# Expert outputs by way of DRAM rows and indirect transfers, in place of scatter products

## The reference

```python
def moe_swiglu(h, w_router, w_gate, w_up, w_down):
    t = h.reshape(-1, d)
    logits = jnp.dot(t, w_router, preferred_element_type=jnp.float32)
    top_val, top_idx = lax.top_k(logits, TOP_K)                      # 2 of 8
    gates = jax.nn.softmax(top_val, axis=-1)
    combine = jnp.sum(jax.nn.one_hot(top_idx, N_EXPERTS) * gates[..., None], axis=1)
    out = jnp.zeros_like(t)
    for e in range(N_EXPERTS):
        out = out + combine[:, e:e + 1] * swiglu(t, w_gate[e], w_up[e], w_down[e])
    return out
```

## Time and profile before

| | us |
|---|---|
| runs | 1451.43, 1448.97, 1451.37 |
| median | 1451.37 |
| profiled execution, span from first to last instruction | 1449.6 |
| PE busy in it | 1406.7 |
| DVE busy | 1159.7 |
| ACT busy | 960.5 |

### The profile page before, as it was taken

One profiled execution on the slowest core, in us unless ns is written; L12 is line 12 of the kernel. 1 busy time (PEld: TensorE's weight loads), 2 busy tenths in 40 slices (PEclk: granted clock), 3 DMA queues, 4 the chain that ended last, 5 costly groups with the idle time before them and its releaser, 6 DMA issues.

```text
span 1449.6 us, 17894 instructions
## 1 busy us (share of the span) xinstructions
PE 1406.7 (97%) x6623; PEld 1155.5 (80%) x6623; DVE 1159.7 (80%) x1063; ACT 960.5 (66%) x841; POOL 9.1 (1%) x51
## 2 busy tenths in 40 slices
PE   7979999999989999999999999999999999999998
PEld 5757788887867888888888888878888888888886
DVE  6884554446686899998898899888889989888986
ACT  5584534344575777777777777767777777777774
POOL 2000000000000000000000000000000000000000
PEclk9999999999999999999999999999999999999999
DMA  8405655365504999999999999989999999999993
GB/s 279 159 30 204 222 183 180 119 232 174 174 8 154 332 380 367 355 377 375 334 353 377 364 358 377 376 297 379 371 366 355 376 358 325 377 377 344 376 369 117
DMA packets 181600, 421.52 MB, mean 291 GB/s; under 512 B 9241, under 2 KB 12365, under 8 KB 181517
## 3 DMA queue, kind: packets, MB, share of 16 engines
q1 hardware_dynamic: 178460, 418.56, 80.5%
q0 software_dynamic: 560, 1.59, 0.4%
q10 hardware_dynamic: 2496, 0.23, 0.1%
HBM read 419.28 MB, written 1.06 MB: 290 GB/s over the span
## 4 chain that ended last, share of the span: by engine, by line
PE 86%; DVE 8%; ACT 3%; issue 2%; DMA 1%; ACTq 0%; DVEq 0%; SPq 0%
PE ps L1753 27%; PE ps L1755 26%; PE ps L1754 26%; PE ps L2211 2%; DVE w_lo L1511 1%; DVE w_lo L1090 1%; DVE work L1199 1%; DVE h L1640 1%; PE ps L2177 1%; ACT w_hi L939 1%; PE ps L2189 0%; PE ps L2188 0%; DMA router<-in_od_router_dram 0%; DMA h<-in_x_dram 0%; ACT w_hi L673 0%
## 5 line engine op out<-in xcount | busy, mean ns | idle before, releaser
L1511 DVE TENSOR_TENSOR w_lo<-raw,w_hi 128x2048 fp32r<-128x2048 f32 x336 | 768.3, 2290 | 105.8 <-ACT w_hi L939 105.1
L939 ACT ACTIVATE w_hi<-raw 128x2048 fp32r<-128x2048 f32 x336 | 644.8, 1919 | 242.7 <-PE ps L1755 242.6
L1753 PE MATMUL ps<-w_hi,xT_hi 128*128 128x512 f32 (+2 forms) x1312 | 514.9, 392 | 10.5 <-DVE w_lo L1090 3.0
L1755 PE MATMUL ps<-w_hi,xT_lo 128*128 128x512 f32 (+2 forms) x1312 | 507.7, 387 | 0.0
L1754 PE MATMUL ps<-w_lo,xT_hi 128*128 128x512 f32 (+2 forms) x1312 | 507.4, 387 | 0.0
L1753 PEld LDWEIGHTS ps<-w_hi,xT_hi 128*128 128x128 f32 x1312 | 247.0, 188 | 64.2 <-issue 6.1
L1755 PEld LDWEIGHTS ps<-w_hi,xT_lo 128*128 128x128 f32 x1312 | 246.8, 188 | 50.6
L1754 PEld LDWEIGHTS ps<-w_lo,xT_hi 128*128 128x128 f32 x1312 | 247.1, 188 | 47.2
L1090 DVE TENSOR_TENSOR w_lo<-raw,w_hi 128x2048 fp32r<-128x2048 f32 (+4 forms) x65 | 138.3, 2137 | 102.4 <-ACT w_hi L673 102.3
L1753 PE MATMUL ps<-w_hi,hT_hi 128*128 128x512 f32 (+1 forms) x548 | 215.4, 393 | 2.0 <-DVE hT_lo L1104 2.0
L1754 PE MATMUL ps<-w_lo,hT_hi 128*128 128x512 f32 (+1 forms) x548 | 213.6, 390 | 0.0
(11 more groups left out here) (288 smaller groups left out, 646.6 us busy)
## 6 DMA issues: line engine op xcount, KB each, us to landing
raw<-in_od_ex_gate_dram SPq DMA_DIRECT2D x112, 1024.0 KB, 5.9
raw<-in_od_ex_up_dram SPq DMA_DIRECT2D x112, 1024.0 KB, 6.0
raw<-in_od_ex_down_dram SPq DMA_DIRECT2D x112, 1024.0 KB, 5.8
raw<-in_od_w_qkv_dram SPq DMA_DIRECT2D x12, 1024.0 KB, 5.4
raw<-in_ev_ff_gate_dram SPq DMA_DIRECT2D x10, 1024.0 KB, 5.4
raw<-in_ev_ff_up_dram SPq DMA_DIRECT2D x10, 1024.0 KB, 5.1
raw<-in_ev_ff_down_dram SPq DMA_DIRECT2D x10, 1024.0 KB, 5.0
raw<-in_ev_w_in_dram SPq DMA_DIRECT2D x5, 1024.0 KB, 9.1
```

The costliest lines, as they stand in the source:

```text
L939: act.activation(w_hi[:, (DENSE + q) % SPLIT, :], raw[:, r, :], ACT.Copy).then_inc(hi_ready, 1)
L1511: dve.tensor_tensor(w_lo[:, k, :], raw[:, raw_of(DENSE + q), :], w_hi[:, k, :].bitcast(F32), ALU.subtract).then_inc(lo_ready, 1)
L1753: pe.matmul(out, x_hi, hi, start=start, stop=False)
L1755: return pe.matmul(out, x_lo, hi, start=False, stop=stop)
```

## The change

Results of experts 0 to 6 no longer pass through scatter products. ACT copies each result from PSUM as plain float32 rows (`y_rows`), and SP stores them to a DRAM table `row_scratch` of 7 x 128 rows, in the next expert ahead of load 12. In expert 0 DVE works out, for each token and each of its two choices, the row number in that table and the weight (`row_places` at step 7, `row_lists` at step 13); the weight is 0 where the choice is expert 7. When the seventh store has landed, in expert 7, POOL issues four indirect transfers (two choices, two halves of the tokens), each of 128 rows of 4 KB, into `hg` and `xs`, which are free by then. DVE adds them into `h` with four operations in expert 7, two at step 24 and two at step 30. Expert 7 itself (and spare runs) still go by selection and scatter products. PE no longer waits for `scatter_read` in the experts, but waits for the copies (`rows_ready`) ahead of an expert's first down unit.

```diff
+ROWS_STORE = 12
+ROWS_ADD = 24
...
+        y_rows = sb("y_rows", [P, D])
+        row_base = sb("row_base", [P, 1, E])
+        row_sums = sb("row_sums", [P, 4, TT])
+        row_index = sb("row_index", [P, 2, TT], I32)
...
+        row_scratch = nc.dram_tensor("row_scratch", (E - 1, P, D), F32, kind="Internal").ap()
...
@@ sync: load_expert @@
                 for q, (kind, j, u) in enumerate(EXPERT):
+                    if q == ROWS_STORE and rows_ahead:
+                        sp.wait_ge(rows_ready, 2 * i)
+                        sp.dma_start(row_scratch[bass.ds(i - 1, 1), :, :].rearrange("e p d -> p (e d)"), y_rows[:, :]).then_inc(rows_stored, 16)
...
@@ scalar @@
+            def output_rows(i, first):
+                act.wait_ge(y_psum, i + 1)
+                if not first:
+                    act.wait_ge(rows_stored, 16 * i)
+                for nn in range(2):
+                    if nn:
+                        act.wait_ge(unit_used, i * len(EXPERT) + (DENSE + len(EXPERT)))
+                    act.activation(y_rows[:, nn * N:(nn + 1) * N], ps[:, 6 + nn, :], ACT.Copy).then_inc(rows_ready, 1)
...
                     for q in range(SPLIT - 1):
                         split_unit(i, q)
-                    outputs(i - 1)
+                    output_rows(i - 1, second)
                     split_unit(i, SPLIT - 1)
...
-                    if q == LAST_UP and even:
-                        turn_selection(p + 1)
+                    if q == LAST_UP and scattered:
+                        turn_selection(1)
...
@@ vector @@
+            def row_places():
+                dve.tensor_scalar(row_base[:, 0, :], slots_f[:, 0:E], float(P), None, ALU.mult).then_inc(vec_chain, 1)
+                chain[0] += 1
+                link(dve.scalar_tensor_tensor(out=g[:, 3, :, :], in0=rank[:, :, 0:E], scalar=float(P), in1=comb[:, :, 0:E],
+                                              op0=ALU.is_lt, op1=ALU.mult))
+                link(dve.scalar_tensor_tensor(out=g[:, 0, :, :], in0=rank[:, :, 0:E], scalar=float(P - 1),
+                                              in1=row_base[:, :, :].to_broadcast([P, TT, E]), op0=ALU.min, op1=ALU.add))
+                for m, hot in enumerate((2, 5)):
+                    dve.tensor_tensor(g[:, 1 + 3 * m, :, :], g[:, hot, :, :], g[:, 0, :, :], ALU.mult)
+                    ins = dve.tensor_tensor(g[:, 7 + m, :, :], g[:, hot, :, :], g[:, 3, :, :], ALU.mult)
+                link(ins)
+            def row_lists():
+                for m in range(2):
+                    dve.tensor_reduce(row_sums[:, m, :], g[:, 1 + 3 * m, :, 0:E - 1], AX.X, ALU.add)
+                    ins = dve.tensor_reduce(row_sums[:, 2 + m, :], g[:, 7 + m, :, 0:E - 1], AX.X, ALU.add)
+                link(ins)
+                dve.tensor_copy(row_index[:, :, :], row_sums[:, 0:2, :]).then_inc(rows_placed, 1)
+            def add_rows(m):
+                dve.wait_ge(rows_back, 16 * 2 * TT)
+                if m:
+                    dve.wait_ge(rows_added, TT)
+                for t in range(TT):
+                    dve.scalar_tensor_tensor(out=h[:, t, :], in0=(hg, xs)[m][:, t, :], scalar=row_sums[:, 2 + m, t:t + 1], in1=h[:, t, :],
+                                             op0=ALU.mult, op1=ALU.add).then_inc(rows_added, 1)
...
                 if begun:
-                    for q in range(SPLIT - 1):
+                    for q in range(SPLIT):
                         split_unit(i, q)
-                    outputs(i - 1)
-                    split_unit(i, SPLIT - 1)
...
+                        if q == 7:
+                            row_places()
...
+                        if q == 13:
+                            row_lists()
...
-                    if begun:
-                        if 1 <= q <= 4:
-                            add_scattered(i - 1, q - 1)
-                        if q == 6:
-                            dve.wait_ge(scatter_read, 4 * i)
+                    if adds and q in (ROWS_ADD, ROWS_ADD + 6):
+                        add_rows((q - ROWS_ADD) // 6)
...
-                        dve.wait_ge(selT_psum, p + 1)
+                        dve.wait_ge(gather_psum, 4 * p + 4)
...
@@ tensor: expert @@
-                    elif begun:
-                        pe.wait_ge(scatter_read, 4 * (i - 1) + 2 + j + 1)
-                    if j == ECH - 1 and even:
-                        pe.wait_ge(selT_ready, p + 1)
+                    if j == ECH - 1 and scattered:
+                        pe.wait_ge(selT_ready, 1)
...
                         pe.wait_ge(hT_ready, i * ECH + j + 1)
+                        if j == 0 and begun:
+                            pe.wait_ge(rows_ready, 2 * i)
...
-                        if j == 1 and u == 0 and begun:
-                            pe.wait_ge(scatter_read, 4 * (i - 1) + (kind == "up") + 1)
...
-                    if q == 1 and begun:
-                        scatter(i - 1, p if even else p + 1, 1 if even else 0)
...
-                    if q == LAST_UP and even:
+                    if q == LAST_UP and scattered:
                         turn_selection(2)
...
-            scatter(E - 1, PAIRS, 1)
+            scatter(0, 1)
...
@@ gpsimd @@
+            pool.wait_ge(rows_placed, 1)
+            pool.wait_ge(rows_stored, 16 * (E - 1))
+            row_table = row_scratch.rearrange("e p d -> (e p) d")
+            for m in range(2):
+                for t in range(TT):
+                    pool.indirect_dma_start((hg, xs)[m][:, t, :], None, row_table,
+                                            bass.IndirectOffsetOnAxis(row_index[:, m, t:t + 1], 0)).then_inc(rows_back, 16)
```

More of the change, by code:

```diff
@@ L424, in trunk @@
         scatter_read = sem("scatter_read")
+        rows_ready = sem("rows_ready")
+        rows_stored = sem("rows_stored")
+        rows_placed = sem("rows_placed")
+        rows_back = sem("rows_back")
+        rows_added = sem("rows_added")
         stored = sem("stored")
@@ L578, in load_expert @@
                     sp.dma_start(dst, src.rearrange("e p k n -> p (e k) n")).then_inc(landed[r], 16)
-            load_expert(0, 0)
+            load_expert(0, 0, False)
             with sp.Fori(1, E) as i:
@@ L591, in spare @@
                     e = sp.value_load(over_i[0:1, n:n + 1], min_val=0, max_val=E - 1)
-                    load_expert(E + n, e)
+                    load_expert(E + n, e, False)
                     if n + 1 < SPARE:
@@ L601, in _ @@
                 v = slice(nn * N, (nn + 1) * N)
-                sp.wait_ge(scatter_read, 4 * (n_over + E) - (3 - n))
+                sp.wait_ge(scatter_read, 4 * (n_over + 1) - (3 - n))
                 sp.dma_start(out[0, t * P:(t + 1) * P, v], h[:, t, v]).then_inc(stored, 16)
@@ L971, in turn_selection, with expert @@
                 act.activation(selT[:, :, :], ps[:, 4, :].rearrange("p (s n) -> p s n", s=2), ACT.Copy).then_inc(selT_ready, 1)
-            def expert(i, even, p, begun, gathers):
+            def expert(i, even, p, begun, gathers, second=False, scattered=False):
                 first = i * len(EXPERT) + DENSE
@@ L1038, in _ @@
             expert(0, True, 0, False, False)
-            expert(1, False, 0, True, True)
+            expert(1, False, 0, True, True, second=True)
             act.wait_ge(routed, 1)
@@ L1044, in _ @@
                 expert(p * 2 + 1, False, p, True, True)
-            expert(E - 2, True, PAIRS - 1, True, False)
+            expert(E - 2, True, PAIRS - 1, True, False, scattered=True)
             expert(E - 1, False, PAIRS - 1, True, False)
@@ L1051, in spare @@
                 with act.If(n_over > n):
-                    turn_selection(PAIRS + n + 1)
+                    turn_selection(n + 2)
                     for half in range(2):
@@ L1626, in gathered_lo, with outputs @@
                                 ps[:, bank:bank + 2, :].rearrange("p b (c n) -> p (b c) n", n=T)).then_inc(x_lo_ready, 1)
-            def outputs(i):
+            def outputs(n):
                 for nn in range(2):
-                    dve.wait_ge(y_hi_ready, 2 * i + nn + 1)
+                    dve.wait_ge(y_hi_ready, 2 * n + nn + 1)
                     v = slice(nn * N, (nn + 1) * N)
                     dve.tensor_tensor(y_lo[:, v], ps[:, 6 + nn, :], y_hi[:, v].bitcast(F32), ALU.subtract).then_inc(y_lo_ready, 1)
+            def row_places():
[22 more added lines that the diff above has]
+                                             op0=ALU.mult, op1=ALU.add).then_inc(rows_added, 1)
             def add_scattered(i, n):
@@ L1638, in add_scattered @@
                 v = slice(nn * N, (nn + 1) * N)
-                dve.wait_ge(scatter_psum, 4 * i + n + 1)
-                dve.scalar_tensor_tensor(out=h[:, t, v], in0=ps[:, 2 + n, :], scalar=comb[:, t, bass.ds(i, 1)], in1=h[:, t, v],
+                dve.wait_ge(scatter_psum, 4 * (i - (E - 1)) + n + 1)
+                dve.scalar_tensor_tensor(out=h[:, t, v], in0=ps[:, 2 + n, :], scalar=comb[:, t, i:i + 1], in1=h[:, t, v],
```

(33 more changed lines are left out.)

2 lines of the change are left out of this document (1 added, 1 removed).

## The result

| | before | after |
|---|---|---|
| median of 4 runs, us | 1450.71 | 1437.78 |
| range, us | 1448.97 to 1451.43 | 1436.20 to 1437.88 |
| profiled execution: its time, us | | 1436.2 |
| its span, us | 1449.6 | 1434.1 |

The ratio of the runs compared is 0.9904, with a 95% interval from 0.9892 to 0.9916: about 1% less time, and the interval excludes 1. The medians lie 12.9 us apart, where 13.6 us were forecast. In the whole study two executions stand far outside, one of the kernel before (2020.76 us) and one with the gathers twice (7888.72 us), and they enter no ratio.

A forecast was written before the change was run, and what follows sets the result against it. PE was taken to set the time: -12.95 (scatters) - 1.29 (turned selections) - 2.5 (waits for h) + 3.0 (sums) + 0.1 (row numbers) = -13.6 us, from the median 1451.37 to 1437.8 us; range 1433 to 1445 us.

The forecast's parts named there:

- PE is the bound, and time off PE counts.: Expert stage: PE loses seven scatters (12.95 us), three turned selections (1.29) and seven waits for h (2.5), counted in full.
- DVE gets less to do, so it doesn't become the pace.: Changes of experts: DVE loses two remainders and four additions, has 102.5 us of gaps; PE's 16.7 us count in full.
- Row numbers.: Expert 0, ahead of prod: DVE's row_places and row_lists, nearly covered by its lead, cost 0.1 us; 1.5 us without cover.
- Sums.: Expert 7, steps 24 and 30: each pair of additions takes 2.4 us against 0.87 us cover; PE stalls 3.0 us altogether.
- Store and gathers at nothing.: Stores behind each expert and four indirect transfers in expert 7 are hidden by the lead of the loads; cost 0.
- the lead shrinks by a few us and holds: Expert 7: with the gathers, 46.7 MB to move; the loads' 9.7 us to spare shrinks slightly but still covers; cost 0.
- landings near 6 us: Sign that the forecast is right: loads still land near 6 us after issue, with SP still waiting for DVE.
- (a): Rival: transfers become the pace, with today's mean of 361 GB/s as the ceiling; about 1467 us, chance 0.04.
- (b): Rival: gathered rows come late in expert 7, holding DVE at step 24, then PE; 1476 us at 25 each, chance 0.06.
- (c): Rival: freed time returns as DVE waits (sums, units 2 or 3, POOL slowing DVE); 4 to 10 us lost, chance 0.13.
- (d): Rival: PE does less, but each change of experts lasts as long, a remainder being late; 1449 to 1452 us, chance 0.05.
- (e): Rival: the sums are covered too and DVE's relief speeds up more; 1431 to 1434.5 us, chance 0.04.

The follow-up runs named there:

- e0: Period of expert 0, from PE's first gather product to ACT's first copy of its result: 123.88 us before, 123.84 after; difference -0.04, forecast -0.33.
- e7: Period of expert 7, from ACT's first copy of the previous result to its first copy into y_hi: 119.54 us before, 120.66 after; forecast difference +0.79.
- e1: Period of expert 1, between ACT's first copies of successive experts' results: 123.84 us before, 121.49 after; difference -2.35, forecast -2.21.
- the idle products: Changed kernel with eight unread products of a scatter's size put back on PE behind unit 1 of experts 1 to 7; 1450.60 us.
- the sums apart: Changed kernel with the four sums of rows one each in steps 22, 28, 34 and 40 instead of two pairs; 1434.44 us.

## Why the prediction was right, and where it was off

The mechanism and the sizes held, but that the median met 1437.8 us to 0.02 us is luck. The forecast counted from 1451.37 us, the median of three runs, and the four runs have 1450.71; and over the expert stage costs 0.62 us above forecast in e0 and e7 stand against gains 0.35 us above it in e1 to e6.

**PE is the bound, and time off PE counts.** Right, and shown: the idle products took back 1.88 us each, up to the time before. The three sizes hold: scatter 1.88 (forecast 1.85), wait for h 0.40 (0.36) and turn 0.40 (0.43), the last two by subtraction.

**"DVE gets less to do, so it doesn't become the pace."** Right, but narrower than it reads. The argument was DVE's 102.5 us of gaps, a sum over the stage. With its old work DVE would have been the pace at each shorter change, for 0.62 us, 4.3 in all. The relief was a condition of the full gain, not a side effect; of the 4.3 us the prediction had counted 2.5, as the waits for h.

**Row numbers.** Forecast 0.1 us. In expert 0 `row_places` stands from 489.59 to 490.55 us ahead of prod, and PE's next unit starts late once, at 493.49 (0.38 us after the product before it, then 0.34, where 0.46 is usual for the two): 0.26 us. With the turn's 0.4 us gone, that leaves most of e0's -0.04 explained, and some 0.1 us not.

**Sums.** The mechanism, the place and the only two stalls were as forecast; the size was 3.4 us against 3.0, the difference being mostly the slower product behind each stall (0.11) and the pair's 2.47 us where 2.4 were taken (the earlier trace rows has 2.5 busy for its two). Shown by the sums apart.

**Store and gathers at nothing.** Right in effect (no gathers: 0.05 us; a second store: none), though the sizes were off, which the time to spare hid. The store lands after 7.0 to 9.3 us, not about 4, since it queues with the loads; a gather lands after 8.9 to 9.8, not 4.2, and its issue takes 2.3 to 2.9, not the 0.53 of the earlier trace rows. Of 63.6 us from the store's issue (1313.82) to the first sum, 27 are used. The step that was too easy is "the lead shrinks by a few us and holds": loads land after 7 us in the median instead of 5.9, and after up to 12.7 us in expert 7, so of the 9.7 us to spare about 3 were left, and double the gathers overran it. The sign "landings near 6 us" did not come.

**Rivals.** (a) is refuted at this size: where the transfers did become the pace they ran at about 400 to 410 GB/s, not at the 361 of the mean before. The Trainium skill's 358 GB/s (HBM Reference, Specifications (TRN2)) is no limit for this core alone, which the same section also says. (b) is a true mechanism that needs rows later by 37 us; forced, it cost 14.4 us. (c) did not come at its price of 4 to 10 us: no unit 2 or 3 was late and POOL didn't slow DVE; its first part came in small, 0.4 us at the sums. (d) is refuted by the periods. (e) did not come, but is what the sums apart reach, at 1434.44.

## What to carry to other kernels

When work is taken off the bounding engine at one place, look there for what its neighbour had been hiding under it: here 0.62 us of DVE a change would have shown, where 0.36 had shown before, had the same edit not taken it away as well. An operation put into an engine's in-order stream should be shorter than that engine's lead at that step; four pieces of 1.28 us were free where two of 2.47 us cost 3.4. A detour through DRAM is free as long as the lead of the other transfers covers it, so look at how late they land against that lead: here landings of 12.7 us of a lead of 15.6 cost nothing, and with 2.1 MB more they reached 17.8 and cost 1.7 us.

## What the runs showed of the hardware

- An indirect transfer of 128 rows of 4 KB cost POOL 0.94 to 1.01 us to issue with DVE standing and 2.27 to 2.90 us beside DVE's remainders, which read two inputs from SBUF; DVE lost nothing.
- A 512 KB store into DRAM, issued among the loads, landed after 8.5 us (median), twice what POOL's 512 KB load had taken in the quieter stretch of the earlier trace rows.
- While PE stood for 13.85 us the granted clock fell to 0.50 (1.2 GHz), and the first products behind it came 0.43 us apart instead of 0.23; in the window from 1405 us it was 1.00 (2.4 GHz) again. After the stalls of 1.4 us it stayed at the higher level, 1.00 from 1380 to 1388 us: products came 0.23 to 0.24 us apart from the second one on.
- One core's stream moved 399 to 409 GB/s in windows of 25 us in which ACT waited for weights (the run with eight stores), and 401 in the changed kernel's window with the gathers.
